# Mixer of the dense blocks: output projection on unscaled halves with the row roots applied at eviction, and 12 modulation jobs moved into FF1 as row dots

## The reference, cut to what matters

```python
# a dense block, for x (and in block 0 for the context)
sh1, s1, g1, sh2, s2, g2 = split(silu(c) @ w_mod[l] + b_mod[l], 6)
o_attn = attention(...)                      # 512 columns
o_conv = silu(layer_norm(conv31(...)) * g + b)   # 512 columns
o = concat([rms(o_attn) * beta_attn[l], rms(o_conv) * beta_conv[l]])
x = x + g1 * (o @ w_o[l])
x = x + g2 * peer(modulate(x, sh2, s2), ...)
# the second block
mod = silu(c_2) @ w_ada + b_ada              # 9 x 1024 values
sh1, sc1, ga1, sh2, sc2, ga2, sh3, sc3, ga3 = split(mod, 9)   # FF1, mixer, FF2
```

## Time and profile before

| what | value |
|---|---|
| median of three runs | 3368.92 us |
| profiled execution: its own time, its span | 3369.91 us, 3368.2 us |
| busy: PE, DVE, ACT, POOL | 91%, 73%, 46%, 28% |
| end of mixer 0 (last write of `XT`) | 370.7 us |
| end of mixer 1 | 1883.7 us |
| FF1: gate and up products, down products | 2688.7 to 2819.9 us, 2820.6 to 2907.7 us |

### The profile page before, as it was taken

One profiled execution on the slowest core, in us unless ns is written; L12 is line 12 of the kernel. 1 busy time (PEld: TensorE's weight loads), 2 busy tenths in 40 slices (PEclk: granted clock), 3 DMA queues, 4 the chain that ended last, 5 costly groups with the idle time before them and its releaser, 6 DMA issues.

```text
span 3368.2 us, 49524 instructions
## 1 busy us (share of the span) xinstructions
PE 3072.9 (91%) x19436; PEld 2693.6 (80%) x19436; DVE 2452.7 (73%) x4855; ACT 1544.5 (46%) x2910; POOL 954.9 (28%) x880
## 2 busy tenths in 40 slices
PE   6998999998999999999888999898999899877898
PEld 4654799998989888888664899898989798744797
DVE  2684489888898688888666588997999745486554
ACT  3454334846557333333444447495555542223443
POOL 0000046555656344433000024456756100000000
PEclk9998999999999999999988999999999899865899
DMA  7387346968879999999437578899999654401344
GB/s 226 100 270 230 107 149 242 335 237 301 284 269 339 368 371 356 365 371 353 130 125 250 173 238 304 301 357 367 380 400 400 250 167 126 138 15 63 125 149 127
DMA packets 372216, 830.20 MB, mean 246 GB/s; under 512 B 20976, under 2 KB 242192, under 8 KB 353424
## 3 DMA queue, kind: packets, MB, share of 16 engines
q1 hardware_dynamic: 274256, 470.32, 40.7%
q0 software_dynamic: 95360, 352.41, 28.6%
q10 hardware_dynamic: 2368, 4.31, 0.4%
HBM read 750.38 MB, written 76.55 MB: 246 GB/s over the span
## 4 chain that ended last, share of the span: by engine, by line
PE 63%; DVE 23%; DMA 7%; ACT 4%; issue 2%; POOL 1%; DVEq 0%; SPq 0%; ACTq 0%; POOLq 0%
PE ps L941 16%; PE ps L588 15%; PE ps L864 14%; DVE fr L1622 6%; DMA ring<-in_peer_v 4%; DVE area L1622 4%; DVE area L1630 3%; PE ps L666 3%; PE ps L920 3%; PE ps L1029 2%; PE ps L605 2%; PE ps L1021 2%; DVE acc L1622 1%; ACT fr L1145 1%; DVE plain L2012 1%
## 5 line engine op out<-in xcount | busy, mean ns | idle before, releaser
L1622 DVE TENSOR_TENSOR fr<-ring,fr 128x1024 fp32r<-128x1024 f32 (+1 forms) x645 | 785.4, 1221 | 515.0 <-ACT fr L1145 511.8
L1145 ACT CAST fr<-ring 128x1024 fp32r<-128x1024 f32 (+1 forms) x681 | 708.4, 1045 | 615.8 <-PE ps L941 324.4
L864 PE MATMUL ps<-fr 128*128 128x384 f32 (+1 forms) x4784 | 856.7, 332 | 16.4 <-DVE fr L1622 16.4
L864 PEld LDWEIGHTS ps<-fr 128*128 128x128 f32 x4784 | 794.1, 193 | 22.6 <-DVE fr L1622 20.2
L941 PE MATMUL ps<-fr 128*128 128x512 f32 x2304 | 524.9, 390 | 4.2 <-DVE fr L1622 4.2
L588 PE MATMUL ps<-fr 128*128 128x256 f32 (+1 forms) x3312 | 482.2, 308 | 30.7 <-DVE fr L1622 30.7
L941 PEld LDWEIGHTS ps<-fr 128*128 128x128 f32 x2304 | 434.2, 189 | 94.7 <-ACT area L1413 4.5
L588 PEld LDWEIGHTS ps<-fr 128*128 128x128 f32 x3312 | 448.5, 194 | 63.4 <-DVE fr L1622 37.3
L2362 POOL DMA_INDIRECT plain<-in_peer_v,area x192 | 275.0, 1432 | 247.0 <-DVE area L1630 166.9
L2394 POOL DMA_DIRECT2D g_scratch<-area x256 | 145.0, 567 | 627.6 <-ACT area L1413 579.6
L966 PE MATMUL ps<-fr 128*128 128x384 f32 x1024 | 301.2, 364 | 19.9 <-DVE fr L1622 18.6
(11 more groups left out here) (204 smaller groups left out, 3936.6 us busy)
## 6 DMA issues: line engine op xcount, KB each, us to landing
ring<-in_peer_uT SPq DMA_DIRECT2D x128, 1024.0 KB, 6.4
ring<-in_peer_v SPq DMA_DIRECT2D x128, 1024.0 KB, 10.7
ring<-in_w_mod SPq DMA_DIRECT2D x48, 1024.0 KB, 6.0
ring<-in_w_ada SPq DMA_DIRECT2D x36, 1024.0 KB, 5.1
w_scratch<-acc POOLq DMA_DIRECT2D x36, 1024.0 KB, 8.3
g_scratch<-area POOLq DMA_DIRECT2D x128, 192.0 KB, 4.8
area<-g_scratch POOLq DMA_DIRECT2D x64, 384.0 KB, 8.7
area<-w_scratch POOLq DMA_DIRECT2D x16, 1536.0 KB, 10.1
```

The costliest lines, as they stand in the source:

```text
L864: ins = e.matmul(o[:, 0:width], pairs[m][0], pairs[m][1], start=(m == 0), stop=(l == 0 and m == last), skip_group_check=l == 1)
L1145: e.copy(hi, x).then_inc(act.after(("high", name)), 1)
L1622: return e.tensor_tensor(o, a, b, op).then_inc(dve.after(*labels), 1)
```

## The change

- `w_o` is cut into 8 units (h, u): half h of the inputs (4 tiles of 128) by 256 outputs. `out_unit` multiplies a unit into two PSUM banks, 24 matmuls. Its inputs are the half multiplied by beta alone, without the root; the high part is written by ScalarE in one activation (`part_high`), the low part by VectorE (`part_low`).
- The roots are turned into a row tile in SBUF (`row`), and VectorE applies gate and root at eviction, then adds to `XT` (`take_out`). Each output tile is evicted once per half.
- In attention's last group, ScalarE makes the high parts and squares of the attention half as its tiles come out. The mean is taken inside attention, at step 33 or 18.
- Jobs: 33 in attention 0 (37 before); 21 in attention 1 as before, now in 18 steps, three of which run two; one after each attention and three in each peer (six and two before).
- 12 of the 84 jobs go: the 24 column tiles that FF2 needs are computed in FF1 as dot products of a row of transposed weights with silu(c_2) broadcast to all partitions (`ada_row`), 12 loads of 1 MB more in FF1's ring order.

```diff
-JOBS = [(kind, m) for kind, n in (("mod0", 48), ("mod1", 48), ("ada", 72)) for m in range(0, n, 2)]
+JOBS = [(kind, m) for kind, n in (("mod0", 48), ("mod1", 48), ("ada", 48)) for m in range(0, n, 2)]
+SIDE_JOBS = ([1] * 33, [2 if n in (3, 8, 13) else 1 for n in range(18)])
+MU_AT = (33, 18)
...
 (sync_program, feed_forward)
             columns(("W", ("gate", n), 256 * c), A[f"w{n}_gate"], 256 * c)
+            if n == 1 and c >= 1:
+                load(("ada", c - 1), A["w_adaT"][c - 1], 2048)
             columns(("W", ("up", n), 256 * c), A[f"w{n}_up"], 256 * c)
+        for j in (10, 11) if n == 1 else ():
+            load(("ada", j), A["w_adaT"][j], 2048)
...
 (tensor_program, mixer)
-        attend(b.at, lambda: mods(1))
+        attend(b.at, beside)
...
+        def out_unit(h, u):
+            name = ("wo", l, h, u)
+            w.wait_ge(*M.low(name))
+            v = M.tile(name, 4)
+            made = [(m, bank(("po", l, h, m), (dve, ("po", l, h, m)))) for m in (2 * u, 2 * u + 1)]
+            for k in range(4):
+                w.wait_ge(dve, ("low", "y", l, 4 * h + k))
+                for i, (m, o) in enumerate(made):
+                    for a, c in ((0, 0), (0, 1), (1, 0)):
+                        ins = e.matmul(o[:, 0:Tq], v[a][:, k, 128 * i:128 * i + 128], HR[:, c, 4 * h + k, 0:Tq],
...
-        squares(("ln", l), 4, Tq, lambda k: M.ACC[:, k, 0:Tq])
-        mods(1)
-        roots(("ln", l), b.rstd, Tq, ("lng", l, 3))
-        mods(1)
-        for h in range(2):
-            squares(("mg", l, h), 4, Tq, lambda k: M.ACC[:, 4 * h + k, 0:Tq])
-            mods(1)
-            roots(("mg", l, h), b.rstd, Tq, ("mh", ("mg", l), h, 3))
-            mods(1)
-        project(("o", l), W4, 1024, Tq, HR, ...
+        mods(1)
+        squares(("mg", l, 0), 4, Tq, lambda k: M.ACC[:, 4 + k, 0:Tq])
+        out_unit(0, 0)
+        roots(("mg", l, 0), b.roots[1], Tq, ("row", l, 0), act)
+        squares(("ln", l), 4, Tq, lambda k: M.ACC[:, k, 0:Tq])
+        out_unit(0, 1)
+        roots(("ln", l), b.roots[0], Tq, ("lng", l, 3))
+        out_unit(0, 2)
+        out_unit(0, 3)
+        squares(("mg", l, 1), 4, Tq, lambda k: M.ACC[:, k, 0:Tq])
+        out_unit(1, 0)
+        roots(("mg", l, 1), b.roots[2], Tq, ("row", l, 1), act)
+        for u in range(1, 4):
+            out_unit(1, u)
...
 (scalar_program, mixer)
+        def part_high(h, k):
+            e.activation(HR[:, 0, 4 * h + k, 0:Tq], b.half(h, k), ACT.Copy, scale=b.beta(h, k)).then_inc(
...
+        def attended(g, i):
+            if g == len(b.streams) - 1:
+                w.wait_ge(act, ("ov", b.at.tag, g, i))
+                part_high(0, i)
+                part_square(0, i)
...
 (vector_program, mixer)
+        def take_out(h, u):
+            w.wait_ge(act, ("row", l, h))
+            made = (2 * u, 2 * u + 1)
+            for m in made:
+                w.wait_ge(pe, ("po", l, h, m))
...
+                for s, (a, z) in b.streams:
+                    stt(b.part[m % 2][:, a:z], ps(("po", l, h, m))[:, a:z], M.MOD[l][:, 16 + m, s:s + 1],
+                        b.rows[h][:, a:z], M_, M_, ("po", l, h, m))
+            for m in made:
+                w.wait_ge(dve, ("po", l, h, m))
+                tt(M.XT[:, m, 0:Tq], M.XT[:, m, 0:Tq], b.part[m % 2], AD, ("xq", l, h, m), ("xo", l, m))
...
 (vector_program, feed_forward)
+        def ada_row(r):
+            w.wait_ge(M.c_in, ("c",))
+            w.wait_ge(*M.here(("ada", r // 2)))
+            x = M.slot(("ada", r // 2), 2048)[:, 1024 * (r % 2):1024 * (r % 2) + 1024]
+            e.scalar_tensor_tensor(out=x, in0=x, scalar=1.0, in1=M.c_all, op0=M_, op1=M_,
+                                   accum_out=M.ADA[:, LATE_ADA + r:LATE_ADA + r + 1]).then_inc(dve.after(("ada", r)), 1)
+            book.freed.setdefault(("ada", r // 2), {})["dve"] = ("ada", r)
...
+            if n == 1 and j >= 5 and j % 2 == 1:
+                ada_row((j - 5) // 2)
         for j in range(len(made) - 4, len(made)):
             take(j)
         if n == 1:
+            for r in range(20, 24):
+                ada_row(r)
```

More of the change, by code:

```diff
@@ L513, in mixer @@
                 jobs(GAP)
-        jobs(M.mixers[l].at.steps)
-        for c0 in W4:
-            columns(("W", ("o", l), c0), A["w_o"][l], c0)
-            if c0 == 0:
-                jobs(3 * GAP)
+        jobs(sum(SIDE_JOBS[l]))
+        src = A["w_o"][l].rearrange("(h k p) m -> h p k m", h=2, p=128)
+        for h in range(2):
+            for c in range(2):
+                load(("Wo", l, h, c), src[h][:, :, 512 * c:512 * c + 512], 2048)
+                if h == c == 0:
+                    jobs(1)
     def peer(l):
@@ L1836, in mixer @@
         tap = taps()
+        step = [0]
         def side():
```

162 lines of the change are left out of this document (124 added, 38 removed).

## The result

The changed kernel takes 3309.85 us (median of 4 runs, 3305.54 to 3315.27), the kernel before 3366.99 (4 runs, 3357.36 to 3374.75): a ratio of 0.983, with a 95% interval of 0.980 to 0.985, or 57 us. A second pair of medians, measured with the last experiments, was 3311.88 against 3366.80, 0.984 (0.982 to 0.987). It is faster; the forecast was 3321, the range 3304 to 3342.

The account below looks back on a forecast made before the run. TensorE was taken as full in most stages, but waiting on chains of sums, roots and spreads in the two dense mixers. -26.8 - 26.6 + 4.1 + 1 = -48.3 from 3369.9 gave 3321.6, stated as 3321; range 3304 to 3342.

Parts of the forecast that it names:

- The end of attention 0: Attention 0's last product ends near 279.6 instead of 280.5: four jobs of 1.6 us go, the mean's 3.7 comes in.
- The tails: From attention's last product to the last write of `XT`; `XT` done 26.8 us sooner in mixer 0, 26.6 in mixer 1.
- The waits: TensorE waits in the mixers: 4.2 us ahead of the first unit and 1.2 ahead of the fifth; mixer 1 2.6, 1.9.
- The new wait for the job's bias: Behind attention 0, VectorE may read the mean only after the job gives it its bias at 280.3, delaying the low parts.
- The half clock: First unit of each mixer, behind TensorE's wait: 7.5 us at half clock, a price of 3.8 us per mixer.
- one of the signs named for being wrong: Half clock in the units of the mixers' second half, which would point to the two rivals about the clock.
- the clock doesn't fall: Rival, both mixers: the new waits pass without half clock, both charges of 3.8 go, 3314 us; chance 0.13.
- stays low: Rival: half clock through all of mixer 1's tail, whose matmul work ends 22 us later, 3344 us; chance 0.10.
- the longer chain: Rival, both mixers: layer norm's spread to the fifth unit's weights takes 5 us more in each, 3332 us; chance 0.10.
- Jobs in attention 1: Three steps with two jobs cost 4.1 us together, the first 2.9 and the others about 0.6 each; bounds 0 and 8.7.
- FF1: 24 row dots and 12 MB more loads, 277 GB/s, cost 1 us more, between 0 and 6.
- The rule of the Trainium skill: Two non-bf16 SBUF sources halve VectorE's throughput: some 4 us more in mixer 0, 2 in mixer 1, forecast near 3327; left aside.

Follow-up runs that it names:

- e5: Changed kernel with its mixer's instructions in TensorE's old order, all three sums and spreads before the eight units: 3340.34 us, 0.991 of before.
- e4: Changed kernel with the attention half's low parts and first unit's low weights ahead of bias and mean, its high weights made in attention: 3303.95 us, 0.981 of before.
- e9: Changed kernel with only the first sum of squares behind each attention computed again, five times in mixer 0, six in mixer 1: 3307.22 us, 0.982 of before.
- e3: Changed kernel with one job in each of attention 1's 21 steps and the mean at the last step: 3310.27 us, 0.983 of before.
- e7: Changed kernel with the first ten tiles of transposed modulation weights loaded twice in FF1: 3329.55 us, 0.988 of before.
- e10: Changed kernel with each of FF1's 24 row dots computed twice, the first result unused: 3322.92 us, 0.987 of before.
- e2: Changed kernel with all 84 jobs, no row dots or extra loads in FF1, and the mean in each attention's last step: 3331.95 us, 0.989 of before.
- e1: Kernel before with only the FF1 part of the change: 72 jobs instead of 84, 12 loads and 24 row dots in FF1: 3354.41 us, 0.996 of before.

## Why the prediction was right, point by point

- *The end of attention 0.* 279.6 forecast, 275.5 and 275.1 measured. The terms named for it (280.5, less four jobs of 1.6, and 3.7 for the mean) give 277.8 and not 279.6; how attention's last steps shorten was not worked out. The profiles of this order lie between 273.6 and 284.1, so the miss is within their spread.
- *The tails.* Right in mechanism and nearly in size: 64.3 and 40.1 us forecast, 61.8 and 37.9 to 39.2 measured, from 90.2 and 66.4. e5 shows that the cover by the products is half of it in mixer 0 and a third in mixer 1. VectorE is not the bound; TensorE waits for no eviction.
- *The waits.* 4.2 forecast and 4.63 measured ahead of the first unit, 1.2 and 1.34 ahead of the fifth in mixer 0; in mixer 1 2.6 and 3.31, 1.9 and 2.26. The new wait for the job's bias was real, and e4 shows what it was worth.
- *The half clock* was the mis-sized term: 3.8 us a mixer forecast, 2.04 and 1.44 measured (7.78 against 5.74, 4.57 against 3.13; 1.26 in mixer 1's second profile). I took 7.5 us at half clock from a stretch of short matmuls; here the clock was full again 4 to 6 us into a dense unit. The prediction also says that every wait longer than 1.77 in the old tails was followed by half clock. That is misread: mixer 1 before had a wait of 2.10 ahead of its last 144 products, and they took 17.54 us, the price of full clock. Its cause was right (e9). In the second profile of the changed kernel the fifth unit of mixer 1 also ran in part at half clock, 4.38 instead of 3.13, behind a wait of 2.25. That is one of the signs named for being wrong, but it cost 1.25 us and not 22. So the rivals in which the clock doesn't fall, or stays low, are out, and with 1.34 and 2.26 ahead of the fifth unit the longer chain too.
- *Jobs in attention 1.* +4.1 forecast, 0 in the trace against e3 (68.44 against 68.42 us). The waits were there (4.0 us), though the first extra job cost 1.17 and not 2.9; the gain of three empty steps at the end was left out of the sum.
- *FF1.* +1 forecast, nothing measured: 116.2 us from the products behind the first pass (2638.59) to the first down product (2754.75), as many as before; 277 GB/s forecast, 267 measured. Its bounds were in the right place: e7 shows where the loads bind, at 308 GB/s and by the ring's slots, e10 that VectorE's room in front of the tables isn't free either.
- *The rule of the Trainium skill* (Vector Engine (DVE) Microarchitecture Reference, "Points that are easy to get wrong") that two non-bf16 SBUF sources halve the throughput: the dots took 1217 ns for 1024 elements, with an accumulator read-out of 81 ns, and the low parts 743 ns for 512 with two SBUF sources, where 742 had one from PSUM. With these, the fp32 forms that the kernel has, the trace does not agree with it, and the forecast of 3327 that hung on it was the further one.
- *What made the difference to 3310*: the three terms, 2 x 3.8 - 3.5 = 4.1 (half clock), 4.1 (jobs) and 1 (FF1), come to 9.2 of the 11 us. That the sum comes so near is in part luck: it leaves out the longer waits (1.6 us the other way in the four places above), the earlier end of attention 0, and peer 1, which took 3 us less than before without a term for it, and it is smaller than the spread of the stages below. The range's upper end, 3342, is also above what the bounds named for it give (3321.6 + 4.6 + 5 + 6 = 3337).

What stays open is the spread of stages that no kernel here touched. Attention 0's last product ended between 273.6 and 284.1 us in the eleven profiles with the changed kernel's steps there, and the stretch from mixer 0's `XT` to attention 1's last product took between 1446.3 and 1455.8 in the ten with its steps there (e3, whose mean stands behind that product, 1444.1). The changed kernel's own two profiles differ by 7.2 us in this stretch. 2.7 of them are there by the end of peer 0's products, 1.6 of it in one wait of TensorE for VectorE's low part (3.66 and 5.22 us); the other 4.5 come in two stretches of short matmuls, 1600 to 1640 and 1700 to 1740, in both of which the granted clock is lower in the second profile. The latter in the two (columns as in the earlier trace rows):

```profile
1700.00:1740.00 40.00, 36.39 (x260) 18.26 (x259) 35.89 (x104) 13.27 (x33) 0.00 (x0) 0.87 0.73 237
```

```profile
1700.00:1740.00 40.00, 38.06 (x236) 20.54 (x239) 31.84 (x92) 11.15 (x28) 0.00 (x0) 0.75 0.67 216
```

The granted clock is 0.87 in the first and 0.75 in the second. What decides it from one execution to the next no run here shows.

## What to carry to other kernels

A scale that is one factor per row can be taken out of the operand and put into the eviction; the product then no longer waits for the chain that makes the scale, and covers it. After such a change look at the first instruction that now releases the products and put everything it doesn't need behind it: here the bias and the mean stood ahead of it, and moving them gave 9 to 14 us with the weights' order, beside the 57 of the change itself. Filler work on the path of a chain is only free while it is shorter than the wait it stands in, at the clock that the wait leaves behind, and while no part of it on another engine (here ScalarE's copy) stands ahead of the chain's next step; and room on an engine is only free if nothing that it holds (a ring slot) is waited for behind it.

## What the runs showed of the hardware

- In these tails a dense unit behind a wait pays for the half clock once and is soon through: 2.04 us behind 4.63 of waiting, 1.58 behind 3.84 (e2), 1.44 behind 3.31. Behind 1.34 it paid nothing in any profile. Behind 2.26 it paid nothing in one execution, and behind 2.25 in another of the same kernel 1.25, and behind 2.92 nothing in e3 and 1.24 in e2. The old products of mixer 1 took 17.54 us behind a wait of 2.10, and 19.04 behind 2.09 in e1. Short pieces between waits don't get out of it: from 1823 to 1857 in the kernel before TensorE was busy 25.9 of 34 us, and the granted clock was 0.52.
- Multiplying without use kept the clock here: sums that nobody reads, over the same wait, had a granted clock of 1.00 and brought the unit from 7.78 to 5.74 us.
- A table load of ScalarE is 1.28 us long and the next activation follows at once:

```profile
306.87 1.28 ACT L1233 ACT_TABLE_LOAD   x1
308.16 0.20 ACT L1233 ACTIVATE scrap<-con 128x1 f32<-128x1 f32 x1
```

The Trainium skill (ScalarE: Activation LUTs, "What ACT_TABLE_LOAD costs") puts a drain of about the same length beside each switch. At this place the trace shows none: ScalarE's last square ends at 306.85, 0.02 us before the load.
